# Weight tiles fetched two to a transfer, into two of the four raw buffers at once, in a hybrid decoder layer

## The reference

```python
def peer(xn, w_pq, sub_keys, expert_u, expert_v):
    ...
    idx = jnp.take_along_axis(cand_i, sel, axis=-1)
    gates = jax.nn.softmax(top_s, axis=-1)
    ...
        pre = jnp.einsum('tkd,td->tk', expert_u[i_blk], x_blk).astype(jnp.float32)
        act = jax.nn.gelu(pre, approximate=False) * g_blk
        return jnp.einsum('tk,tkd->td', act.astype(x_blk.dtype), expert_v[i_blk])
```

## Time and profile before

| | before |
|---|---|
| median of 3 runs | 2121.04 us |
| profiled execution, its own time | 2123.82 us |
| its span (first to last instruction) | 2122.0 us |
| TensorE busy | 2051.0 us, 97% |
| VectorE busy | 1635.8 us, 77% |
| ScalarE busy | 1082.9 us, 51% |
| mean granted TensorE clock | 0.983 |
| moved by DMA | 496.19 MB, mean 234 GB/s |

### The profile page before, as it was taken

The page is one execution under the profiler, slowest core; times in us unless marked ns, Lnnn a source line. Parts: engine busy times, 40 slices in busy tenths (PEclk is TensorE's granted clock), DMA queues, the critical chain, the costliest instruction groups (busy, mean ns, idle before and its releaser), DMA issues.

```text
span 2122.0 us, 38323 instructions
## 1 busy us (share of the span) xinstructions
PE 2051.0 (97%) x12266; PEld 1879.2 (89%) x12266; DVE 1635.8 (77%) x2501; ACT 1082.9 (51%) x1450; POOL 722.4 (34%) x423
## 2 busy tenths in 40 slices
PE   7999999879999999999999989999999999999997
PEld 7888778878789999999999989999999899999785
DVE  6885776985557888888888656889889788888755
ACT  6543566234434755545554544555555555555454
POOL 0030200000000878788888860222222233333000
PEclk9999998999999999999999999999999999999998
DMA  5755558206555777777777776899999889999453
GB/s 200 254 178 179 178 174 312 70 33 217 187 178 169 211 207 206 212 208 207 206 213 207 213 218 240 308 351 344 349 347 340 294 303 334 359 334 337 158 179 139
DMA packets 171858, 496.19 MB, mean 234 GB/s; under 512 B 48624, under 2 KB 49040, under 8 KB 169872
## 3 DMA queue, kind: packets, MB, share of 16 engines
q1 hardware_dynamic: 117056, 413.39, 56.5%
q0 software_dynamic: 51200, 67.25, 12.1%
q10 hardware_dynamic: 3536, 14.78, 1.9%
HBM read 476.31 MB, written 19.04 MB: 233 GB/s over the span
## 4 chain that ended last, share of the span: by engine, by line
PE 82%; DMA 8%; DVE 5%; ACT 2%; issue 1%; DVEq 1%; ACTq 0%; SPq 0%
PE ps L260 27%; PE ps L265 14%; PE ps L1880 13%; PE ps L1885 7%; DMA raw<-in_v_table 6%; PE ps L286 5%; PE ps L280 5%; PE ps L281 5%; DVE lo L240 2%; ACT hi L234 1%; DMA arena<-in_u_table,few_index 1%; PE ps L1775 1%; PE ps L362 1%; PE ps L1783 1%; PE ps L1731 1%
## 5 line engine op out<-in xcount | busy, mean ns | idle before, releaser
L234 ACT ACTIVATE hi<-raw 128x1024 fp32r<-128x1024 f32 x724 | 767.4, 1061 | 874.7 <-PE ps L260 405.0
L240 DVE TENSOR_TENSOR lo<-raw,hi 128x1024 fp32r<-128x1024 f32 x724 | 891.6, 1235 | 357.4 <-ACT hi L234 328.9
L260 PE MATMUL ps<-act_pair,hi 128*128 128x448 f32 (+1 forms) x2816 | 655.9, 375 | 5.7 <-ACT hi L234 5.7
L1618 POOL DMA_INDIRECT gate_map<-gate_in_sb x256 | 473.5, 1850 | 409.9 <-DVEq L1383 334.3
L260 PEld LDWEIGHTS ps<-act_pair,hi 128*128 128x128 f32 x2816 | 505.6, 189 | 55.2 <-ACT hi L234 5.9
L265 PEld LDWEIGHTS ps<-act_pair,lo 128*128 128x128 f32 x2816 | 372.4, 191 | 18.7 <-DVE lo L240 3.6
L265 PE MATMUL ps<-act_pair,lo 128*128 128x224 f32 (+1 forms) x2816 | 375.7, 276 | 1.7 <-DVE lo L240 1.7
L1880 PE MATMUL ps<-stage,hi 128*128 128x448 f32 x1024 | 233.0, 369 | 3.4 <-ACT hi L234 1.9
L1880 PE MATMUL ps<-act_pair,hi 128*128 128x448 f32 x1024 | 229.6, 366 | 1.0 <-ACT hi L234 1.0
L1635 POOL DMA_INDIRECT arena<-in_u_table,few_index x64 | 100.1, 1564 | 318.9 <-DVE keep L1433 276.8
L1880 PEld LDWEIGHTS ps<-stage,hi 128*128 128x128 f32 x1024 | 183.7, 189 | 18.5 <-issue 2.8
(11 more groups left out here) (253 smaller groups left out, 1683.1 us busy)
## 6 DMA issues: line engine op xcount, KB each, us to landing
raw<-in_expert_u SPq DMA_DIRECT2D x256, 512.0 KB, 3.5
raw<-in_v_table SPq DMA_DIRECT2D x256, 512.0 KB, 6.7
raw<-in_w_in_cols SPq DMA_DIRECT2D x64, 512.0 KB, 3.2
raw<-in_w_in_rows SPq DMA_DIRECT2D x48, 512.0 KB, 3.3
raw<-in_w_out SPq DMA_DIRECT2D x32, 512.0 KB, 3.3
raw<-in_w_pq SPq DMA_DIRECT2D x32, 512.0 KB, 3.3
raw<-in_w_gate SPq DMA_DIRECT2D x32, 512.0 KB, 3.8
gate_map<-stage SPq DMA_DIRECT2D x1, 14336.0 KB, 41.1
```

Of the source, the lines that this page charges most:

```text
L234: act.activation(hi[:, use, :], raw[:, slot, :], ACT.Copy).then_inc(hi_ready, 1)
L240: dve.tensor_tensor(lo[:, use, :], raw[:, slot, :], hi[:, use, :].bitcast(F32), ALU.subtract).then_inc(lo_ready, 1)
L260: mm = pe.matmul(first_tokens(out_ap), hi[:, use, d8 * P:(d8 + 1) * P], first_tokens(act_pair[:, d, :]), start=(d == 0), stop=False)
L1618: pool.indirect_dma_start(gate_map, bass.IndirectOffsetOnAxis(ap=place[0:n, unit, r:r + 1], axis=0), gates_out[0:n, unit, r:r + 1], None, ...
```

## The change

Loads go out two tiles at a time. `load_pair` takes an even tile n and writes tiles n and n+1 into slots n mod 4 and the next with one transfer of 1 MB (two runs of 4 KB in each partition). It waits until both slots are free: `lo_ready` at n-2 or more, that is, until tile n-3 has left its buffer. There are two semaphores for landed weights, one for each pair of slots, and ACT waits on the pair's for either tile.

```diff
-        weights_landed = [sem(f"weights_landed{i}") for i in range(RAW)]
+        weights_landed = [sem(f"weights_landed{i}") for i in range(RAW // 2)]
...
-        def load_tile(sp, n, slot, src, first=False):
+        def load_pair(sp, n, slot, pair, first=False):
             if not first:
-                sp.wait_ge(lo_ready, n - RAW + 1)
-            sp.dma_start(raw[:, slot, :], src).then_inc(weights_landed[slot], 16)
+                sp.wait_ge(lo_ready, n - RAW + 2)
+            sp.dma_start(raw[:, slot:slot + 2, :], pair.rearrange("a p f -> p a f")).then_inc(weights_landed[slot // 2], 16)
 
         def round_tile(act, n, slot, use, turn, first=False):
-            act.wait_ge(weights_landed[slot], 16 * turn + 16)
+            act.wait_ge(weights_landed[slot // 2], 16 * turn + 16)
...
-            for k in range(RAW):
-                load_tile(sp, k, k, w_in_cols[k], first=True)
+            for k in range(0, RAW, 2):
+                load_pair(sp, k, k, w_in_cols[k:k + 2], first=True)
...
-                    for k in range(RAW):
+                    for k in range(0, RAW, 2):
                         n, slot, _, _ = tile_at(base, i, RAW, k)
-                        load_tile(sp, n, slot, source[ds(i * RAW + k, 1)].rearrange("a p f -> (a p) f"))
+                        load_pair(sp, n, slot, source[ds(i * RAW + k, 2)])
...
-                for k in range(RAW):
+                for k in range(0, RAW, 2):
                     n, slot, _, _ = tile_at(T_V + CHUNKS * half, j, RAW, k)
-                    load_tile(sp, n, slot, v_tiles[half][ds((j + moved) * RAW + k, 1)].rearrange("a p f -> (a p) f"))
+                    load_pair(sp, n, slot, v_tiles[half][ds((j + moved) * RAW + k, 2)])
```

## The result

The changed kernel takes 2254.75 us (median of 4 runs, 2248.12 to 2256.64) against 2122.74 us: the ratio is 1.0612, with a 95% interval of 1.0592 to 1.0631. That is +132 us; the forecast was +100, within 2130 to 2350.

What follows compares the result with a forecast made beforehand. TensorE, busy for 97% of the span, was taken as the bound. Value stage +98, U stage +1 and start +1 us sum to +100: 2224 us profiled, 2221 us as median of the runs, range 2130 to 2350 us.

Steps and rivals of the forecast that it cites:

- The bound and the place: Whole kernel: TensorE bounds; the loss falls in the value stage, where loads have 0.5 and 1.0 us to spare per loop.
- The hold: Value stage: time from landing to the next load's issue grows from 2.67 to 5.19 us (first half) and 4.76 (second).
- Landing of a pair, first half: Value stage, first half: a 1 MB load lands in 7.0 us, making 3.05 us per tile, +64 us.
- Landing of a pair, second half: Value stage, second half: a 1 MB load lands in 6.5 us, making 2.815 us per tile, +34 us.
- the even exchange: Value stage: the pair's second half adds 1.6 us, offset by no longer queueing behind the preceding load; single-tile median kept.
- The rule against the loss: Value stage: the skill's 1 MiB batching and fit give 4.4 us per pair, loops under TensorE's, so zero loss.
- U stage: U stage: pair lands in 5.4 us, loop 10.11 against 10.09 us, just covered, +1 us, hardly any wait for loads.
- The other stages: Input projection and other projections: loop 8.9 against 11.2 us, covered; the start costs +1 us.
- Mild: Value stage: emptier queues let a pair land in 5.8 us, +38 us, about 2159; chance 0.15.
- severe: Value stage: pair queues like the 2 MB load, +232 us, and U stage +55, up to 2408; chance 0.13.
- Nothing: Value stage: a pair lands within 5.0 us, so no loss, 2121 us; chance 0.09.
- faster: Value stage: fewer transfers land sooner and ScalarE's 92 waits vanish, giving back 6.4 us, about 2114; chance 0.05.

Runs made afterwards that it cites:

- bunched gathers: Changed kernel with at most two gathers under way in the value stage's second half instead of four: 2262.07 us, ratio 1.0627 to the kernel before.
- both waits: Kernel before with single 512 KB loads, both issued when both buffers are free, and ScalarE waiting for both tiles: 2313.58 us, ratio 1.0855.
- when alone: Changed kernel with pair loads everywhere but in the value stage, which has single loads as before: 2133.67 us, ratio 1.0051 to the kernel before.
- Each of the two waits alone: Kernel before, single loads: even tile's load issued one tile later, 2203.46 us; or ScalarE waiting for both tiles before rounding the even one, 2211.0 us.

## Why the prediction was right

The forecast was 34 us low. Nearly all of that is one term of the sum, the landing of a pair in the second half; the mechanism, loads that come too late for the loop of the buffers, was right.

- *The bound and the place.* Right. 126.5 of 132 us arose in the value stage, whose cover was put at 0.5 and 1.0 us. The U stage stayed at 2.51 us per tile.
- *The hold.* Right within 0.2 us. From landing to the next issue it is H with 0.17 us ahead of it (the chain's 1565.51 to 1565.68) and 0.17 behind: 5.22 us in the first half (5.19 forecast), 4.92 in the second (4.76).
- *Landing of a pair, first half.* 7.0 us forecast, 7.02 - 0.17 = 6.85 us measured: +64 forecast, +61 measured. That the pair's second half would cost just what its place in the queue gives back was an argument, not a measurement; it came out here, and no run shows that it had to.
- *Landing of a pair, second half.* This is the mis-sized term: 6.5 us taken from the single loads' median, 7.62 - 0.17 = 7.45 until ScalarE could start (a landing of 7.3), and +34 forecast where +66 came. The step that failed is the even exchange, 1.6 us for the pair's own second half against 1.6 us no longer spent behind the preceding load. In landings, single against pair, it held in the first half (6.8 and 6.9 us), where a gate map load also stood in the queue, and not in the second (6.5 and 7.3). What sets the 0.85 us is open. Without gathers 0.4 of it stays (5.3 and 5.7 us); with the table tiled and the gathers there, 0.1 (6.3 and 6.4). So neither the gathers nor the rows make all of it alone, and bunched gathers are not the cause (7.55 against 7.62 us). Nor was the number of gathers varied by itself; VectorE asks for 0.60 per tile there from tile 147 of the stage on, against 0.47 in the first half.
- *The rule against the loss.* The Trainium skill's rule of 1 MiB or more per transfer ("DMA: Bandwidth & Descriptors", Bandwidth), taken with its fit, forecast no loss. For the transfer alone it points the right way: 53 us given back against two single loads under the same waits. It leaves out that with a fixed number of buffers the larger transfer brings both waits, 185 us here. The Trainium skill's fit ("DMA: Bandwidth & Descriptors", Anatomy of one DMA), which it gives for transfers issued by GpSimd and by which I estimated 4.4 us for a pair, was short by 2.5 us and more in this stage; in the input projection a pair landed in 4.7.
- *U stage.* Forecast at +1 us, just covered. Right in time, and just: TensorE was busy for 498.6 of the 500 us. The sign I gave, hardly any wait for loads, was wrong: ScalarE waited 93.2 us for weight loads between 700 and 1200 us, before the change not at all. I had also summed over the 198 tiles of that stretch and not the stage's 256, which makes the forecast's +1 no larger than +1.3.
- *The other stages.* Forecast 1 us, measured 10 us when alone. The step "covered, as in the other projections" looked at each stage's steady loop and not at single large transfers in the queue. About 3.4 us come from the constants at 96 us, where a stall also lowered the clock, and about 3 us around the start of the U stage (4.0 between tiles 176 and 200, some of it regained). There ScalarE goes over to another activation function and back in each four tiles, and the reload of its table, 1.28 us, comes only when the pair has landed, so it lies in the loop:

```profile
718.74 1.28 ACT L234 ACT_TABLE_LOAD   x1 [2.62 <-DMA raw<-in_expert_u]
```

This pair landed at 718.6 us and was rounded from 720.04; tile 192, its first, is where the delay grew most, by 2.4 us. In the kernel before, that tile had landed before ScalarE turned to it. That the reload is the cause is read from this trace and was not tested by a run. The first tile's delay at the start, 0.9 us, was gone by tile 4.

- *Rivals.* "Mild" and "severe" named the two sides of the landing time. Of "severe" one part came: I had written that a fall of the granted clock in the value stage would make the forecast wrong, and it fell, to 0.98 and 0.96 in the two stretches. It carries little: 0.02 x 340 + 0.04 x 400 = 23 us of TensorE time at most, part of it in time in which TensorE would have waited, and the loop of the loads gives the measured time per tile without it. "Nothing" and "faster" are excluded by the interval of 1.0592 to 1.0631.

## What to carry to other kernels

Merging two transfers into one with a fixed number of buffers means that buffers are freed and filled two at a time. Before it, compare the loop of a buffer (landing under the traffic of that stage, plus the hold until the last of the merged tiles is free) with what the bounding engine needs for all buffers; here the cover was 0.5 to 1.0 us and the hold grew by 2.3 to 2.6. Take the landing time from the busiest stage, and look at one-off large transfers in the same queues, for they find the thinned cover too.

## What I had not expected of the hardware

- One transfer of 1 MB is worth more than two of 512 KB issued back to back: 6.1% over the kernel before, against 8.6% with the same waits, and ready 7.02 us after the first issue instead of 8.33.
- With no gathers beside it, a 512 KB tile read from rows 1 MB apart still landed in 5.1 to 5.7 us. With all gathers, laying the table out tile by tile brought a pair 0.9 us (7.02 to 6.17 in the first half) and a single tile only 0.2 to 0.3.
- Each of the two waits alone costs 79 and 87 us, both together 185: neither hides behind the other, and the cover is used up once.
